# The picks of the gathered tokens in two halves, none between the key lists, and a lead of 10 pairs instead of 12

## What is computed

```python
def peer_ffn(hn, wq, sub_keys, u, v):              # 8 heads, 2 x 128 keys each, 16 picks a head
    q = (hn @ wq).reshape(bsz, seq, 8, 2, 128)
    sc = jnp.einsum("bshpc,hpnc->bshpn", q, sub_keys)
    v1, i1 = lax.top_k(sc[..., 0, :], 16)
    v2, i2 = lax.top_k(sc[..., 1, :], 16)
    cand = (v1[..., :, None] + v2[..., None, :])   # 256 candidates a head
    top, ci = lax.top_k(cand, 16)
    idx = e1 * 128 + e2                            # e1, e2: i1, i2 at ci // 16, ci % 16
    g = jax.nn.softmax(top, axis=-1)               # 128 picks a token
    a = jnp.einsum("td,ted->te", xb, u[idx]); w = g * gelu(a)
    return jnp.einsum("te,ted->td", w, v[idx])
```

## Time and profile before

| | us |
|---|---|
| median of three runs | 4155.15 (4152.26 to 4163.14) |
| the profiled execution | 4161.85 |
| its span in the profile | 4160.0 |
| busy: TensorE | 3970.9 (95%) |
| busy: VectorE | 2840.4 (68%) |
| busy: ScalarE | 1691.3 (41%) |
| busy: GpSimd | 1359.6 (33%) |

### The profile page before, as it was taken

One profiled execution on the slowest core, in us unless ns is written; L12 is line 12 of the kernel. 1 busy time (PEld: TensorE's weight loads), 2 busy tenths in 40 slices (PEclk: granted clock), 3 DMA queues, 4 the chain that ended last, 5 costly groups with the idle time before them and its releaser, 6 DMA issues.

```text
span 4160.0 us, 59372 instructions
## 1 busy us (share of the span) xinstructions
PE 3970.9 (95%) x19746; PEld 3404.5 (82%) x19746; DVE 2840.4 (68%) x4322; ACT 1691.3 (41%) x3102; POOL 1359.6 (33%) x898
## 2 busy tenths in 40 slices
PE   7998999989999999999999989999799999999998
PEld 5666887779999988888766678877799999888786
DVE  1684351599988977777717843417998889677776
ACT  2522123224666654333424221322256666434343
POOL 5344563411211432222243345733112124322231
PEclk9999999989999999999999999999999999999999
DMA  3112332227878999999711123312368789999995
GB/s 123 50 60 75 104 105 67 92 78 248 297 268 300 374 368 350 348 350 344 269 69 46 56 86 106 117 61 87 125 233 300 273 286 402 372 353 341 336 349 189
DMA packets 360974, 879.45 MB, mean 211 GB/s; under 512 B 27856, under 2 KB 191952, under 8 KB 353872
## 3 DMA queue, kind: packets, MB, share of 16 engines
q1 hardware_dynamic: 153360, 508.20, 34.2%
q0 software_dynamic: 73728, 268.47, 17.1%
q10 hardware_dynamic: 133696, 100.67, 8.0%
HBM read 774.47 MB, written 102.76 MB: 211 GB/s over the span
## 4 chain that ended last, share of the span: by engine, by line
PE 71%; DVE 14%; issue 4%; DVEq 4%; DMA 3%; ACT 2%; ACTq 1%; POOL 1%; SPq 0%; POOLq 0%
PE ps L1169 41%; PE ps L1464 21%; PE ps L1441 3%; DVE wlo L776 1%; DVE conv L832 1%; DMA raw<-in_experts 1%; PE ps L1177 1%; DVEq L794 1%; DVE ubuf L1031 1%; DVE acc L1038 1%; DMA act_e<-early_gelu 1%; DVEq L952 1%; PE ps L1217 1%; PE ps L1315 1%; PE ps L1235 1%
## 5 line engine op out<-in xcount | busy, mean ns | idle before, releaser
L1169 PE MATMUL ps<-xhi,whi 128*128 128x384 f32 (+1 forms) x3328 | 1227.2, 369 | 117.2 <-DVE xlo L790 31.5
L1169 PE MATMUL ps<-xlo,whi 128*128 128x384 f32 (+1 forms) x3328 | 1194.9, 359 | 0.0
L1169 PE MATMUL ps<-xhi,wlo 128*128 128x384 f32 (+1 forms) x3328 | 1194.8, 359 | 0.0
L1169 PEld LDWEIGHTS ps<-xhi,whi 128*128 128x128 f32 x3328 | 633.6, 190 | 195.7 <-issue 69.9
L459 ACT ACTIVATE whi<-raw 128x1024 fp32r<-128x1024 f32 x610 | 638.8, 1054 | 321.6 <-PE ps L1464 241.4
L776 DVE TENSOR_TENSOR wlo<-raw,whi 128x1024 fp32r<-128x1024 f32 x512 | 622.6, 1220 | 160.0 <-ACT whi L459 156.0
L1169 PEld LDWEIGHTS ps<-xlo,whi 128*128 128x128 f32 x3328 | 634.3, 191 | 52.5 <-issue 5.3
L1169 PEld LDWEIGHTS ps<-xhi,wlo 128*128 128x128 f32 x3328 | 633.0, 190 | 53.0
L419 POOL DMA_INDIRECT ubuf<-in_up_rows,gidx x256 | 290.1, 1133 | 1120.7 <-DVE small L1031 929.6
L1464 PE MATMUL ps<-whi,eh 128*128 128x512 f32 x1536 | 601.7, 392 | 27.3 <-DVE el L1130 27.3
L1464 PE MATMUL ps<-whi,el 128*128 128x512 f32 x1536 | 600.1, 391 | 0.0
(11 more groups left out here) (200 smaller groups left out, 4803.9 us busy)
## 6 DMA issues: line engine op xcount, KB each, us to landing
raw<-in_experts SPq DMA_DIRECT2D x512, 512.0 KB, 6.3
raw<-in_back SPq DMA_DIRECT2D x112, 512.0 KB, 3.2
gate_table<-gbuf SPq DMA_DIRECT2D x48, 1024.0 KB, 8.9
act_e<-early_gelu ACTq DMA_DIRECT2D x128, 384.0 KB, 7.1
gtile<-gate_table ACTq DMA_DIRECT2D x30, 1536.0 KB, 23.5
raw<-in_front SPq DMA_DIRECT2D x64, 512.0 KB, 3.2
raw<-in_gates SPq DMA_DIRECT2D x48, 512.0 KB, 3.2
early_gelu<-weighted SPq DMA_DIRECT2D x128, 192.0 KB, 5.7
```

Of the source, the lines that this page charges most:

```text
L1169: ins = MM(out, w[:, a:a + P], x[:, c, t0:], start=(i == 0 and n == 0), stop=(i == len(chunks) - 1 and n == 2))
```

## The change

- The eight picks between the lists are gone. Token block 0's picks come in two halves of four heads: `pick(0, 0..7)` at the start of the lead, then the row numbers and gaps of this half (`row_numbers(0)`); `pick(0, 8..15)` in the first eight halves of row block 0, then `row_numbers(1)`. Exponents and shares are taken half by half, and `gidx_ready` counts two a layer.
- The picks of token block 2 no longer stand one in each half of row block 0: four stand in its first eight halves, twelve in its last eight. So row block 0 has 24 steps of `pick` instead of 16. Block 1 is as before.
- The lead has 10 pairs (`LEAD`), with two low halves after every third pick. Behind the row blocks follow four pairs instead of two (the 17th of block 2 and `TRAIL` = 3).
- Gathered picks: one a half in blocks 0 and 1, 28 in block 2 instead of 32, one with each of the four pairs at the end.
- The last gate loads: one load of 16 to 24 after pair 61, instead of 16 to 22 after pair 62 and 22 to 24 behind the last store; the first `load_acts` stand behind it, and two pairs follow.

```diff
-LEAD = 12
+LEAD = 10
-assert LEAD + DB * BLOCK + 1 == EARLY
-SELS_OF = (1, 1, 2)
-SEL_EARLY = sum(SELS_OF) * HALVES
+TRAIL = EARLY - LEAD - DB * BLOCK
+def spread(n, items):
+    return [n * (k + 1) // items - n * k // items for k in range(items)]
+SELS_OF = [1] * (2 * HALVES) + spread(28, HALVES) + [1] * (TRAIL + 1)
+PICKS = ((0, 0), (1, None), (0, 1), (2, None), (3, None))
+SLOT_OF = (0, 1, 1, 0)
...
                 for i in range(LEAD):
                     early_pair(i)
-                    if i == 2 or i == LEAD - 3:
-                        pick_weights(int(i > 2))
+                    if i == 3:
+                        pick_weights(0, 0)
                     if i == LEAD - 2:
+                        pick_weights(1)
                         pick_turn(1)
...
+                        if b == 0 and k == 8:
+                            pick_weights(0, 1)
...
-                    else:
-                        gates_stored(L, 11)
-                        load_gates(L * 0, 0, 16, 22)
+                for k in range(TRAIL + 1):
+                    early_pair(EARLY - TRAIL - 1 + k, sels(DB * HALVES + k))
+                    if k == 1:
                         gates_stored(L, 12)
-                        load_gates(L * 0, 0, 22, 24)
+                        load_gates(L * 0, 0, 16, 24)
                         load_acts(L * 0, 0)
                         load_gates(L * 0, 1)
                         load_acts(L * 0, 1)
-                        early_pair(i + HALVES + 1)
...
+                def row_numbers(part):
+                    a = part_of(part)
+                    drain()
+                    STT(out=eidx[:, 2, a], in0=eidx[:, 0, a], scalar=float(NK), in1=eidx[:, 1, a], op0=ALU.mult, op1=ALU.add)
+                    pick_gaps(0, part)
+                    drain()
+                    TS(gidx[:, a], eidx[:, 2, a], base_col, None, ALU.add).then_inc(gidx_ready, 1)
...
                 for l in range(LISTS):
...
-                    if 4 <= l < 12:
-                        pick(0, l - 4)
...
-                for t, k in [(0, k) for k in range(LISTS // 2, HALVES)] + [(1, k) for k in range(HALVES)]:
+                for t, k in [(0, k) for k in range(HALVES // 2)] + [(1, k) for k in range(HALVES)]:
...
-                    if n == 12:
-                        pick_shares(0, gsel[:, :])
+                    if n == 14:
+                        pick_shares(0, gsel[:, part_of(0)], 0)
...
+                H = HALVES // 2
+                second = [[(0, H + k)] + {1: [(2, 0)], 3: [(2, 1)], 5: [(2, 2), (2, 3)]}.get(k, []) for k in range(H)]
+                third = [[(2, H // 2 + n) for n in range(3 * k // 2, 3 * (k + 1) // 2)] for k in range(H)]
+                PIECES = (second + third, [[(3, k)] for k in range(HALVES)], [[]] * HALVES)
...
-                        if b + 1 < DB:
-                            pick(b + 2, k)
-                        else:
-                            drain()
+                        for t, p in PIECES[b][k]:
+                            pick(t, p)
+                            if (t, p) == (0, HALVES - 1):
+                                row_numbers(1)
+                        if b == 0 and k == 9:
+                            pick_shares(0, gsel[:, part_of(1)], 1)
+                        drain()
```

More of the change, by code:

```diff
@@ L64 @@
 HALVES = 2 * GROUPS
-LEAD = 12
+LEAD = 10
 BLOCK = HALVES + 1
 EARLY = PAIRS
-assert LEAD + DB * BLOCK + 1 == EARLY
-SELS_OF = (1, 1, 2)
-SEL_EARLY = sum(SELS_OF) * HALVES
+TRAIL = EARLY - LEAD - DB * BLOCK
+assert LEAD % 2 == 0 and TRAIL > 0
+def spread(n, items):
+    return [n * (k + 1) // items - n * k // items for k in range(items)]
+SELS_OF = [1] * (2 * HALVES) + spread(28, HALVES) + [1] * (TRAIL + 1)
+SEL_EARLY = sum(SELS_OF)
+FIRST_SEL = [sum(SELS_OF[:k]) for k in range(len(SELS_OF) + 1)]
+HALF = SEL // 2
+assert SEL_EARLY == HALF
+PICKS = ((0, 0), (1, None), (0, 1), (2, None), (3, None))
+SLOT_OF = (0, 1, 1, 0)
 GB = 4
@@ L226, in build_trunk, with part_of @@
         base_col = small[:, 60:61]
+        def part_of(part):
+            return slice(0, SEL) if part is None else slice(part * HALF, (part + 1) * HALF)
         GATE_BANK0 = (0, 4, 5)
@@ L700, in _ @@
                     shares(b, 0)
-                    for _ in range(SELS_OF[b]):
+                    for e in sels(b * HALVES):
                         coef(e)
-                        e += 1
                     for k in range(HALVES):
-                        new = range(e, e + SELS_OF[b]) if k + 1 < HALVES else range(e, e)
-                        early_pair(i + k, new)
-                        e = new.stop
+                        early_pair(i + k, sels(b * HALVES + k + 1) if k + 1 < HALVES else ())
                         row_copies(b, k)
@@ L1001, in pick_shares @@
+                def pick_shares(t, out, part=None):
+                    n = PH if part is None else PH // 2
+                    p3 = picks2[SLOT_OF[t]][:, part_of(part)].rearrange("p (h k) -> p h k", k=TOPK)
+                    dve.wait_ge(pick_exp, L * len(PICKS) + PICKS.index((t, part)) + 1)
+                    V.tensor_reduce(small[:, 48:48 + n], p3, AX.X, ALU.add)
                     drain()
-                    V.reciprocal(small[:, 40:48], small[:, 48:56])
+                    V.reciprocal(small[:, 40:40 + n], small[:, 48:48 + n])
@@ L1091, in _ @@
                         onehots(b, k)
-                        new = range(e, e + SELS_OF[b])
+                        new = range(FIRST_SEL[b * HALVES + k], FIRST_SEL[b * HALVES + k + 1])
                         for x in new:
@@ L1097, in _ @@
                         axpys(old)
[L1098 to L1102 removed]
+                        old = new
+                        for t, p in PIECES[b][k]:
[4 more added lines that the diff above has]
+                            pick_shares(0, gsel[:, part_of(1)], 1)
+                        drain()
                     if b + 1 < DB:
[L1104 removed]
                         pick_gaps(b + 2)
[L1106 to L1108 removed]
+                        low(2 * (i + HALVES))
+                        low(2 * (i + HALVES) + 1)
                         pick_shares(b + 2, eidx[:, 2, :]).then_inc(pick_ready, 1)
[L1110 to L1111 removed]
+                for k in range(TRAIL + 1):
+                    i = EARLY - TRAIL - 1 + k
+                    new = range(FIRST_SEL[DB * HALVES + k], FIRST_SEL[DB * HALVES + k + 1])
+                    low(2 * i)
+                    for x in new:
+                        dot(x)
+                    low(2 * i + 1)
+                    axpys(old)
+                    old = new
+                    drain()
+                e = SEL_EARLY
                 def by_group(x):
@@ L1445, in _ @@
                         turn(b + 2)
-                early_pair(EARLY - 1, 1, EARLY // 2 - 1)
+                for i in range(EARLY - TRAIL, EARLY):
+                    early_pair(i, i % 2, i // 2)
                 pe.wait_ge(g_copied, (L + 1) * (DB * P // 4))
```

52 lines of the change are left out of this document (25 added, 27 removed).

## The result

The changed kernel takes 4166.46 us (median of 20 runs, 4159.12 to 4174.6), the kernel before 4152.52 us (20 runs, 4146.55 to 4163.14). The ratio is 1.0033 with a 95% interval of 1.0026 to 1.0039: **0.33% slower, 13.9 us**. The forecast was 4149.9, slightly faster. The time lies inside the range of 4136 to 4167, at its upper end, but on the other side of no change than the forecast.

The account below looks back on a forecast made before the run. VectorE was taken to pace the lead, TensorE row block 0, with a hole of 8.75 us before the down phase. 2 x (0 + 1.25 + 0.9) + 1.0 = 5.3 us off 4155.15 gave 4149.9, range 4136 to 4167.

Parts of the forecast that it names:

- Lead and block 0 together: 0: Stretch from the key lists to the second turn: gains and losses cancel; bounds 5.0 us better, 2.6 worse a layer.
- the join: Between last pair and down phase: stall 4.2 plus 3.3, 7.5 us instead of 8.75, so 1.25 us gained a layer.
- block 2: Third row block: 28 gathered picks instead of 32 may remove TensorE's 3.1 us wait; 1.0 us gained in all, bounds 0 and 3.1.
- block 1: Second row block: taken as untouched by the change, with no gain or loss.
- the gain of the down phase's clock: Start of the down phase: smaller holes before it keep the granted clock higher, 0.9 us gained a layer, bounds 0 and 2.0.
- VectorE's work in block 0: First row block: halves, 24 picks, row numbers and shares were summed to 171.1 us of VectorE time.
- the held queue: Rival, chance 0.12: ScalarE sits 20.6 us issuing loads before the down phase, pair 63 waits; 15.5 us slower, 4170.7.
- VectorE slips more in block 0: Rival, chance 0.05: late gathered rows cost 0.5 us a half in the first row block, 8 us a layer; 4165.9.
- VectorE keeps ahead: Rival, chance 0.08: in the first row block VectorE doesn't delay TensorE; 5.0 us more gained a layer, 15.3 in all, 4139.9.
- the join closes: Rival, chance 0.2: ScalarE's hold before the down phase is near 7.2 us, clock stays up; 17.4 us faster, 4137.8.
- A wait for raw panels in the last four pairs: Sign of being wrong, in the pairs behind the row blocks: expected absent, though the gathers now don't stop there.

## Why the prediction was wrong

**The step that failed** is "Lead and block 0 together: 0". It measured +6.9 and +6.5 us in the two layers, 13.4 in all. A second term failed too: the join was to gain 2.5 us over both layers and lost 7.1. What hid a part of this was luck: block 2 gained 7.6 us where I had 1.0. So the time came out 19.2 us from the sum (13.9 slower instead of 5.3 faster), of which the first term makes 13.4, the join 9.6, block 1 1.2 and block 2 -6.6; 1.6 stays over, for the most part the gain of the down phase's clock, which these stretches leave out. The parts of the first term, layer 0:

- *Up to the start of block 0 it held.* VectorE left the lists at 887.6 (forecast 887.2), the turn came at 975.45 (974.6), the one-hots at 977.6 (977.0). The lead gained 3.2 and 2.1 us instead of 5.2. In layer 0 the two pairs between turn and rows took 18.6 us, at a granted clock of 0.91, instead of 17.05. This hardly counts, since VectorE sets the second turn. In layer 1 they took 19.8 us (0.85), and there it did count: VectorE waited 1.2 us for a coefficient of ScalarE, and its stretch up to the last pick was 176.8 us instead of 175.6. With a lead of 12 the two pairs took 17.05 us in both layers, at 1.00, and the stretch 175.6.
- *VectorE's work in block 0 was taken 4.5 us too small.* The sum said 171.1; it was 175.6 (977.6 to 1153.2). The halves' drains would be 2.9 of it, 16 times the 0.18 us by which the halves differ (10.10 and 9.92); the run with a drain less took 173.2 us (975.92 to 1149.17), so they cost 2.4. The diff shows this line (`drain()` outside the `else`); I had read it as the old one. Two short waits are 0.4 of the rest; the other 1.7 us I can't name.
- *The hand-over from VectorE's last pick to the 17th pair* took 2.8 us (1153.2 to 1156.04) instead of 1.9. I had 0.3 us for the exponent, and no table loads. With the exponent one pair later it took 1.7 us in both layers, so this is a cost of 1.1.
- *The 17th pair* took 1.6 us more than 8.33, at a granted clock of 0.83. I had no clock term in this place. In layer 1 it took 8.43 us at 1.00, and that layer lost 6.5 us all the same.

So the second turn came 7.6 us later than forecast: 0.6 for the one-hots' start, 4.5, 0.9 and 1.6. From this, 0.4 goes off because the lists ended later, and 0.3 that I had kept back. TensorE's waits in block 0, 4.5 us for low halves and 2.2 for the gelu, are near the "some 5 us" forecast: the mechanism, VectorE as the bound of block 0, was right, and its size was short.

**What lies under it.** My sum set 21.9 us won (4.6 of them the low halves of the two pairs) against 16.7 us for the two pairs, and took the pairs as a given part of the change, without asking what they cost in each place. The lead is bound by VectorE, where a pair costs 2.35 us, its two low halves together; behind the rows it costs TensorE's 8.33. By the prediction's own numbers the two pairs thus cost 16.7 - 4.6 = 12.1 us a layer, and the rest of the change had to earn that back. The runs show both sides: the halves and the free lists alone, with 12 pairs, are worth 6.9 us a layer; taking two pairs out of the lead alone costs 13.7 and 14.9; together they make the +6.9 and +6.5 of the change. So the gain of the change was real and was spent.

**Block 2** gained 5.5 and 2.1 us; I had 1.0 in all (bounds 0 and 3.1). In layer 0, 3.1 of it are waits that went, and 2.4 are matmuls that ran faster: the same ones kept TensorE busy 164.7 us before (granted clock 0.99) and 162.3 after (1.00). TensorE lost its waits there in every version with 26 to 30 picks in this block, while the run that kept 32 still takes 166.4 and 164.6 us there (after: 162.3). That the fewer gathers did it is the likeliest reading, not separately tested.

**The join** was to gain 1.25 us a layer, and the clock of the down phase 0.9; the join lost 2.9 and 4.2. Pair 63 waited 6.2 and 6.9 us instead of 4.2, since from the first issue at 1517.47 to the release at 1531.2 it took 13.7 us instead of 11.1. The hole behind it is 3.3 us as forecast. Together 9.5 replace 8.75. The clock then fell in pair 63 itself (10.48 us instead of 8.34, and 11.24 in layer 1), a term that I didn't have. The gain that I had put on the clock did come, in the down phase: its first 24 matmuls took 7.18 and 7.15 us instead of 8.06 and 7.51. Loading the second tile late removed the wait of pair 63, as the held queue says. Of the rivals, "the held queue" had the right place and sign but not the size (hold 20.6, stall 13.7), and "VectorE slips more in block 0" came nearest: it priced the slip at 8 us a layer (measured 6.9 and 6.5), but put it down to late rows, where the runs show drains, the exponent's table loads and the clock. That its time, 4165.9, nearly meets the measured one is luck: it keeps the gain at the join, which was a loss, and has no gain in block 2. "VectorE keeps ahead" and "the join closes" are excluded by the waits. A wait for raw panels in the last four pairs, one of the signs of being wrong, doesn't stand in the trace.

**Block 1** was to stay and lost 0.6 us a layer, the same drain: without it the 0.55 went.

## What to carry to other kernels

Before work is moved between stages, price it on the engine that bounds each stage: a pair of the lead cost 2.35 us there and 8.33 elsewhere. Here a lead that shrank while VectorE still bound it only made waits: 8.3, 18.0 and 26.6 us of them with 12, 10 and 8 pairs. When VectorE sets the end of a stretch, count its drains and everything between its last operation and TensorE's next, on every engine passed. Keep large loads out of the queue in which an evacuation stands, or issue them behind it: here that took away a wait of 6.2 us.

## What the hardware showed unexpectedly

- Each change between exponent and gelu on ScalarE shows a table load of 1.28 us in these rows, twice for one exponent of 0.31 us. The Trainium skill, page "ScalarE: Activation LUTs", section "What ACT_TABLE_LOAD costs", gives about 1283 ns for the load, which the rows show, and a drain of 1380 ns with it, which they don't: the gelu at 1155.42 starts right behind the load that began at 1154.13.
- ScalarE's sequencer was held for 11.74 us in one DMA issue with 2432 KB of loads ahead, against 4.00 with 2048 KB ahead; with 1536 KB less it was 1.57 us for two issues. The hold nearly tripled for a fifth more to load, so the amount alone doesn't set it; the panels and gathers in flight with it are the likely rest, not tested.
- The granted clock fell to 0.83 in the pair behind a wait of 2.19 us (and some shorter ones in block 0), in layer 0 of the changed kernel and in both layers of the lead of 8. Behind a wait of 2.1 or 2.2 us at the same place it stayed at 1.00 in layer 1 of the changed kernel and in both layers of the kernel with the second gate tile late and of the lead of 12. Pair 63 took 10.48 us behind a wait of 6.2.
